# The SwiGLU block of a two-layer hybrid decoder in two phases: gate and up with stationary weight tiles, then down over all of K

## What is computed

```python
h = rms_norm(x, attn_norm_w[l])
proj = h @ w_in[l]
...
x = x + concat([attn, ssm]) @ w_out[l]
h = rms_norm(x, ffn_norm_w[l])
ff = (silu(h @ w_gate[l]) * (h @ w_up[l])) @ w_down[l]
x = x + ff
```

## Time and profile before

| | |
|---|---|
| time, three runs | 2185.56, 2186.34, 2186.9 us |
| median | 2186.34 us |
| span of the profiled execution | 2184.5 us |
| TensorE busy | 2165.0 us (99%), 10150 matmuls |
| VectorE, ScalarE, GpSimd busy | 58%, 46%, 5% |
| DMA read from HBM | 388.43 MB, 179 GB/s over the span |

### The profile page before, as it was taken

One profiled execution on the slowest core, in us unless ns is written; L12 is line 12 of the kernel. 1 busy time (PEld: TensorE's weight loads), 2 busy tenths in 40 slices (PEclk: granted clock), 3 DMA queues, 4 the chain that ended last, 5 costly groups with the idle time before them and its releaser, 6 DMA issues.

```text
span 2184.5 us, 29947 instructions
## 1 busy us (share of the span) xinstructions
PE 2165.0 (99%) x10150; PEld 1794.3 (82%) x10150; DVE 1272.9 (58%) x1542; ACT 1004.1 (46%) x1284; POOL 111.1 (5%) x159
## 2 busy tenths in 40 slices
PE   9999999999999999999999999999999999999998
PEld 7888888888888888888878887888888888888887
DVE  5866765455555555555567666555555555555555
ACT  5555654444444434444355556544444444344442
POOL 2023100000000000000000232000000000000000
PEclk9999999999999999999999999999999999999999
DMA  6554356666656556665545533565665555666654
GB/s 217 174 164 135 116 174 188 192 193 193 190 189 189 189 192 192 192 187 189 174 147 182 159 122 127 182 192 187 191 193 190 191 189 188 191 192 192 187 189 153
DMA packets 202813, 391.55 MB, mean 179 GB/s; under 512 B 12224, under 2 KB 12592, under 8 KB 202736
## 3 DMA queue, kind: packets, MB, share of 16 engines
q1 hardware_dynamic: 201952, 388.67, 55.9%
q0 software_dynamic: 784, 1.90, 0.3%
HBM read 388.43 MB, written 2.10 MB: 179 GB/s over the span
## 4 chain that ended last, share of the span: by engine, by line
PE 97%; ACT 1%; issue 1%; DVE 0%; SPq 0%; POOL 0%; DMA 0%; DVEq 0%; ACTq 0%; POOLq 0%
PE ps L458 91%; PE ps L467 3%; PE ps L557 1%; PE ps L506 0%; PE ps L621 0%; PE ps L620 0%; PE ps L593 0%; PE ps L594 0%; PE ps L619 0%; POOL ys L424 0%; PE ps L565 0%; PE ps L562 0%; PE ps L548 0%; ACT w_hi L770 0%; DMA vrows<-in_k_norm_w_dram 0%
## 5 line engine op out<-in xcount | busy, mean ns | idle before, releaser
L1003 DVE TENSOR_TENSOR w_lo<-raw,w_hi 128x1024 fp32r<-128x1024 f32 x736 | 905.7, 1232 | 739.0 <-ACT w_hi L985 544.4
L985 ACT CAST w_hi<-raw 128x1024 fp32r<-128x1024 f32 x480 | 506.7, 1056 | 739.4 <-PE ps L458 739.4
L458 PE MATMUL ps<-w_hi,h_hi 128*128 128x512 f32 x1984 | 624.0, 396 | 3.6 <-DVE h_lo L1012 3.5
L458 PE MATMUL ps<-w_hi,h_lo 128*128 128x512 f32 x1984 | 613.3, 390 | 0.0
L458 PE MATMUL ps<-w_lo,h_hi 128*128 128x512 f32 x1984 | 612.4, 390 | 0.0
L458 PEld LDWEIGHTS ps<-w_lo,h_hi 128*128 128x128 f32 x1984 | 373.3, 188 | 79.0
L458 PEld LDWEIGHTS ps<-w_hi,h_lo 128*128 128x128 f32 x1984 | 373.3, 188 | 78.8
L458 PEld LDWEIGHTS ps<-w_hi,h_hi 128*128 128x128 f32 x1984 | 366.5, 188 | 75.1 <-DVE w_lo L1003 4.4
L770 ACT CAST w_hi<-raw 128x1024 fp32r<-128x1024 f32 x256 | 269.9, 1055 | 199.9 <-PE ps L458 193.5
L458 PE MATMUL ps<-w_hi,m_hi 128*128 128x512 f32 x960 | 297.2, 391 | 2.6 <-DVE m_lo L1194 2.6
L458 PE MATMUL ps<-w_hi,m_lo 128*128 128x512 f32 x960 | 295.8, 389 | 0.0
(11 more groups left out here) (181 smaller groups left out, 852.5 us busy)
## 6 DMA issues: line engine op xcount, KB each, us to landing
raw<-in_w_gate_dram SPq DMA_DIRECT2D x176, 512.0 KB, 3.5
raw<-in_w_up_dram SPq DMA_DIRECT2D x176, 512.0 KB, 3.5
raw<-in_w_down_dram SPq DMA_DIRECT2D x176, 512.0 KB, 4.3
raw<-in_w_in_dram SPq DMA_DIRECT2D x144, 512.0 KB, 3.4
raw<-in_w_out_dram SPq DMA_DIRECT2D x64, 512.0 KB, 4.2
out_dram<-xr SPq DMA_DIRECT2D x4, 512.0 KB, 2.8
xr<-in_x_dram POOLq DMA_DIRECT2D x3, 512.0 KB, 6.7
xr<-in_x_dram SPq DMA_DIRECT2D x1, 512.0 KB, 4.4
```

The lines of the kernel that those rows point to most:

```text
L458: done = nc.tensor.matmul(ps[:, bank + t, :], lhs[:, rows + k, t * P:(t + 1) * P], w[:, slot, k, :], start=(first and k == 0 and w is w_hi ...
L985: nc.scalar.copy(w_hi[:, s, :, :], raw[:, s, :, :]).then_inc(hi_split, 1)
L1003: v_.tensor_tensor(w_lo[:, slot, :, :], raw[:, slot, :, :], w_hi[:, slot, :, :].bitcast(F32), ALU.subtract).then_inc(lo_split, 1)
```

## The change

- **Gate and up** are formed for all 11 chunks first. The weight tile of 128x128 is stationary and 256 columns of h (all tokens) move: products_turned, 24 matmuls of 256 columns for a pair. The result comes out with inner columns on partitions, so turn_ff and its PSUM use are gone.
- rs now lies along the free axis: two transposes per layer spread it over all partitions (spread_rs), ACT copies it to rsb. DVE multiplies gate by rsb (scale_gate), ACT applies SiLU in place (silu_gate), DVE multiplies up by it (form_ff), ACT copies to f_hi and DVE forms f_lo, each 128x1024. The factor rs of up is applied at the end, when the down sum is added (add_down).
- f_hi and f_lo hold 44 tiles each for all of K. The attention's buffers and m_hi, m_lo lie in the same memory.
- **Down** follows: four output chunks, 22 pairs each, summed over all of K in PSUM, added to x once per output chunk.
- The next layer's transposes of vrows and of x's first three chunks stand between the down pairs, the fourth behind pair 1 of the next layer. SP loads the next layer's parameter rows a chunk before the down phase, and stores each output chunk but the last between the loads of the one after.
- Layers and chunks are written out without hardware loops; thresholds are constants. Each product group alternates between banks 0, 1 and 2, 3 in one count over both layers (bank_of).

```diff
-    P_LOOP = P_FF + 2 * PPG
-    DOWN = DCH * CT // 2
-    PER_FF = 2 * PPG + DOWN
-    P_LAST = P_LOOP + (FCH - 1) * PER_FF
-    PAIRS = P_LAST + DOWN
+    FT = FF // P
+    PER_FF = 2 * PPG
+    P_DOWN = P_FF + FCH * PER_FF
+    DOWN = FT // 2
+    PAIRS = P_DOWN + DCH * DOWN
...
+            def products_turned(slot, pair, rows, bank, first, last):
+                pe.wait_ge(lo_split, pair + (1 + RING))
+                for k in range(2):
+                    for h, w in ((h_hi, w_hi), (h_lo, w_hi), (h_hi, w_lo)):
+                        for m in range(CT):
+                            done = nc.tensor.matmul(ps[:, bank + m // 2, m % 2 * TOK:(m % 2 + 1) * TOK],
+                                                    w[:, slot, k, m * P:(m + 1) * P], h[:, rows + k, :],
...
+                done.then_inc(pair_used, 1)
...
+            def spread_rs(layer):
+                pe.wait_ge(rs_ready, layer * 2 + 2)
+                for t in range(T):
+                    last = nc.tensor.transpose(ps[:, 6, t * P:(t + 1) * P], rs[:, t:t + 1].broadcast_to([P, P]),
+                                               ident[:, :])
+                last.then_inc(rsb_psum, 1)
...
+                for n in range(DCH):
...
                     for q in range(DOWN):
...
+                        if n == 0 and q % 2 == 0:
+                            pe.wait_ge(ff_lo, layer * FCH + (q // 2 + 1))
+                        products(q % RING if n % 2 == 0 else (q + 2) % RING, base + (P_DOWN + n * DOWN + q), 2 * q,
+                                 down_bank(layer, n), f_hi, f_lo, q == 0, q == DOWN - 1)
+                        if layer + 1 < DEPTH and n == 0 and q == 0:
+                            turn_vecs(layer + 1)
+                        if layer + 1 < DEPTH and n and q == 1:
+                            if n == 2:
+                                pe.wait_ge(vec_ready, layer + 2)
+                            turn_x(layer + 1, 0, n - 1)
...
+            def ff_high(layer, c):
+                act.wait_ge(ff_ready, layer * FCH + c + 1)
+                nc.scalar.copy(f_hi[:, CT * c:CT * (c + 1), :],
+                               stage[:, 1].rearrange("p t (a c) -> p (t a) c", a=2)).then_inc(ff_hi, 1)
...
+            def scale_gate(layer, c):
...
+                dve.wait_ge(pair_used, layer * PAIRS + (P_FF + c * PER_FF + PPG + RING))
+                at = gate_bank(layer, c)
+                v_.tensor_tensor(by_tile(stage[:, 0]), by_tile(ps[:, at:at + 2, :]),
+                                 rsb[:, :].unsqueeze(1).broadcast_to([P, CT, TOK]), ALU.mult).then_inc(gate_scaled, 1)
...
+            def form_ff(layer, c):
+
+                dve.wait_ge(pair_used, layer * PAIRS + (P_FF + (c + 1) * PER_FF + RING))
+                dve.wait_ge(gate_silu, layer * FCH + c + 1)
+                at = up_bank(layer, c)
+                v_.tensor_tensor(stage[:, 1], ps[:, at:at + 2, :], stage[:, 0], ALU.mult).then_inc(ff_ready, 1)
```

More of the change, by code:

```diff
@@ L14 @@
+import math
 from contextlib import ExitStack
@@ L255, in load_pair @@
                     .then_inc(raw_landed[slot], 16)
[L257 to L298, removed]
@@ new lines, in _ @@
+            for layer in range(DEPTH):
+                for p in range(PAIRS):
+                    load_pair(p % RING, layer * PAIRS + p, source(layer, p))
+                    if layer == 0 and p == 1:
+                        load_rows(0)
+                    if layer + 1 < DEPTH and p == P_DOWN - PER_FF:
+                        load_rows(layer + 1)
+                    if layer == DEPTH - 1 and p >= P_DOWN + DOWN and (p - P_DOWN) % DOWN == 8:
+                        store((p - P_DOWN) // DOWN - 1)
@@ L351, in _ @@
             pool.memset(numbers[:, 7:8], 0.0).then_inc(const_ready, 1)
-            with pool.Fori(0, DEPTH) as layer:
-                one = bass.ds(layer, 1)
+            for layer in range(DEPTH):
+                one = slice(layer, layer + 1)
                 for dst, src in ((dtb, dt_bias), (alog, a_log), (dskip, d_skip), (sink, sinks)):
@@ L793, in squares @@
                 else:
-                    own.done(layer, ins)
+                    own.done(ins)
             def x_square(layer, i):
@@ L892, in g_hi, with rsb_out @@
                 turned_hi(m_hi, 8 + CT * z, 4, V_SSM + CT * z, gT_psum, layer * 4 + (2 * z + 1), mg_hi)
[L894 to L907 removed]
+            def rsb_out(layer):
+                act.wait_ge(rsb_psum, layer + 1)
+                nc.scalar.copy(rsb[:, :], ps[:, 6, 0:TOK]).then_inc(rsb_ready, 1)
@@ new lines, in _ @@
+            act.wait_ge(vec_psum, 1)
+            own.done(nc.scalar.copy(vecs[:, :], ps[:, 6, 0:VROWS]))
+            nc.scalar.mul(qw[:, :], vecs[:, V_Q:V_Q + 1], HEAD ** -0.5).then_inc(vec_ready, 1)
+            x_hi(0, 0, 0)
+            split(1)
+            x_hi(0, 0, 1)
+            split(2)
+            for layer in range(DEPTH):
+                base = layer * PAIRS
+                for p in range(PAIRS):
+                    if base + p + LEAD < ALL:
+                        split(base + p + LEAD)
+                    if layer == 0 and p in (0, 2):
@@ L990, in _ @@
-                ff_high(layer * 2 * FCH + 2 * FCH - 1)
-                for p in range(P_LAST + LEAD, PAIRS):
-                    split(layer, p)
-            own.check()
+                        x_chunk_squares(layer, 1, (p - 82) // 8)
+                    if P_FF <= p < P_DOWN:
+                        c, q = (p - P_FF) // PER_FF, (p - P_FF) % PER_FF
+                        if c == 0 and q == PPG:
+                            rsb_out(layer)
+                        if q == (PPG + 2 if c == 0 else PPG):
+                            silu_gate(layer, c)
+                        if c and q == 0:
+                            ff_high(layer, c - 1)
@@ new lines, in ff_low @@
+            def ff_low(layer, c):
+                dve.wait_ge(ff_hi, layer * FCH + c + 1)
+                tiles = slice(CT * c, CT * (c + 1))
+                v_.tensor_tensor(f_lo[:, tiles, :], by_tile(stage[:, 1]), f_hi[:, tiles, :].bitcast(F32),
+                                 ALU.subtract).then_inc(ff_lo, 1)
+            split_lo(0)
+            x_lo(0, 0, 0)
+            split_lo(1)
+            x_lo(0, 0, 1)
+            split_lo(2)
+            for layer in range(DEPTH):
+                base = layer * PAIRS
+                for p in range(PAIRS):
```

458 lines of the change are left out of this document (236 added, 222 removed).

## The result

The changed kernel takes **2234.22 us** (median of 4 runs, 2233.18 to 2234.27) against 2186.11 us of the kernel before beside it. The ratio is 1.022, 95% interval 1.0206 to 1.0235: slower by 2.2%, 48 us, where 2158 us was forecast. The profiled execution has a span of 2232.4 us.

A forecast was written before the change was run, and what follows sets the result against it. TensorE, busy 99% of the span, was taken as the bound. 2184.5 - 22.7 - 6.4 + 0.6 + 0.1 = 2156.1 us span; with the runs' median 1.84 us above the span, 2158 us, range 2152 to 2174.

The forecast's parts named there:

- the first term: Gate and up turned: 8448 matmuls of 256 columns cost the same as 4224 of 512, 0 us added.
- turn_ff goes: FFN chunks: eight transposes per chunk leave PE, with the waits at each layer's end, -22.7 us together.
- the boundary: Between the layers: the stall for h_lo and the slow-clock first pair go, transposes stand between down pairs, -6.4 us.
- spread_rs: Two added transposes per layer on PE, with the changes of matmul kind around them, +0.6 us.
- the tail: Last down group: its sum now also multiplies by rs, 747 for 684 ns, twice, +0.1 us.
- the wait at the last chunk: End of each layer's FFN: PE idles 1.28 us for m_lo; with transposes and slow restarts 2.43 us, twice, saved.
- DVE, ACT and the leads: FFN: DVE and ACT stay near half busy, splits run three pairs ahead of PE, so nothing is added.
- The pace of pairs: Gate and up: matmuls 113 to 114 ns apart; prediction wrong if 24 short matmuls take over 2.8 us.
- the short stream can't be fed: Every gate and up chunk: instruction supply can't keep up, 118 ns a matmul, 39 us more, 2197 us; chance 10%.
- pair starts cost: Gate and up: each pair of 24 short matmuls pays 0.03 us at its start, +10.6 us, 2169 us; chance 16%.
- loads bare: Gate and up: each of 4224 added 188 ns weight loads stands on the path, 794 us, 2950 us; chance 1%.
- Exchanges quicken: Attention stages: constant thresholds take away PE's 3.6 us of waits, 2154 us; chance 7%.

The follow-up runs named there:

- experiment 10: Kernel before with each 512-column product made as two of 256 with the same stationary tile: 2294.26 us, ratio 1.0499.
- experiment 4: Changed kernel with f_hi and f_lo moved 96 bytes lower, to a multiple of 128 bytes: 2212.4 us, ratio 1.0124 to the kernel before.
- Experiment 7: Changed kernel with f at a multiple of 128 bytes, but gate and up formed unturned as before: 2175.79 us, ratio 0.9958 to the kernel before.
- experiment 3: Kernel of matmul blocks alone on TensorE, varying address phases and column counts: 128, 320 and 384 columns took 110.8, 146.6 and 174.4 ns.

## Why the prediction was wrong

**The step that failed** is the first term: "So each load lies under the matmul before it, the columns set the pace, and 8448 x 113.35 = 4224 x 226.7: nothing added." Two readings fitted one row. The 512-column pace of 226.7 ns is 213.3 ns of columns at 2.4 GHz and 13.4 ns more; I read these as proportional to the columns because dt_products came out at exactly half. They are a fixed price for each matmul with its load, which four numbers of columns and experiment 10 show. dt_products at 113.3 were in a steady pace that they hold in one kernel and not in another: 118.4 ns in experiment 10, at the same addresses. Gate and up never had it. What chooses that pace stays open. The arithmetic that should have raised doubt stood in the trace: 226.7 less 512 columns leaves 13.4 ns, and a fixed price would have given 120 ns and +56 us. I had bounded this term by +10.6 us beside the forecast and by +39 us in a rival with 10%. The term measured **+56.2 us** for 0.

**A term that was missing.** The diff puts f_hi at 229344 - 2 * FT * TILE, 32 bytes past a multiple of 64 and 96 bytes out of phase with w_hi, and m_hi and m_lo on it. I priced this edit at nothing without naming it. It measured **+22 us** (experiment 4), for w_out as well, which the change does not touch otherwise.

**Point by point.**
- *turn_ff goes, the boundary, spread_rs, the tail: -28.4 us.* Right in sum. With f in phase the changed kernel is 27.8 us above the kernel before, and 56.2 - 28.4 is 27.8; the interval of that comparison is about 4 us to either side, so the exact match is luck. Experiment 7 singles out the boundary and the wait at the last chunk: 9.5 us expected, 8.7 measured (6.3 to 12.2 by the interval). The transposes of turn_ff follow by difference, and no run takes them out alone.
- *DVE, ACT and the leads.* Right: PE waits for no split in the FFN, and DMA releases none of ACT's but the kernel's first.
- *The pace of pairs.* The prediction's own test failed as it said it would: 24 short matmuls take 2.88 us, over the 2.8 named.
- *Rival: the short stream can't be fed (10%).* The side was right, and its price of 118 ns near, but not its mechanism. Matmuls of 128 columns with their loads come every 110.8 ns (experiment 3), so the supply can do at least that. The pace is 120.0 in a block of 96 alone, grows with the columns at 2.4 GHz, and changes to 117.8 with 64 bytes of address.
- *Rival: pair starts cost (16%).* Out as the cause: the blocks alone have no pairs and no waits in them and run at 120.0.
- *Rival: loads bare.* Out: in gate and up PEld is busy 480.00 of 480 us and PE as well, and 120.0 is far from 188 more. The Trainium skill ("TensorE: Matmul & The Clock Gate", Part 3, The mechanism) states that a weight load overlaps running matmuls only when the row groups differ. This trace does not agree: loads of all rows overlap, and what is left on the path is 13.3 ns.
- *Exchanges quicken, at most 3.6 us.* Hardly: PE's waits there are 3.2 us for 3.6. The argument against it, that most end on another engine's work, holds by their number, but 1.9 of the 3.6 us were "issue". The sum of the terms is 1.8 us above the measured span, which is within what the runs of the kernel before differ by.

The mechanism beneath stays open. The pace depends on the phase between the two operands' addresses, 226.7 or 233.3 ns at 512 columns, 120.0, 118.6 or 117.8 at 256. That may point to something that both share, and no run here shows what. The Trainium skill ("TensorE: Matmul & The Clock Gate", Part 2, Step-by-step) says that loading the next tile's weights takes no read bandwidth from the running matmul. No run here measures that bandwidth; that the distance of the two operands' addresses changes the pace by 6.6 ns at 512 columns is not what one would expect from it.

## What to carry to other kernels

Count matmuls and their weight loads as well as columns: in this number format each matmul with its load took about 13 ns beside the columns, so turning a product to save a transpose must not halve the columns per load. Test a pace that is to be multiplied by thousands against two column counts before using it, since one short block may sit in a pace of its own: here the same 32 matmuls ran at 113.3 ns in one kernel and at 118.4 in another. Watch the start addresses of matmul operands, moving and stationary, whenever buffers move: 64 bytes were worth 1% here, in a kernel whose code was the same.

## What the runs showed that was not expected

- In phase (both operands' start addresses the same modulo 256 bytes) a matmul with its own load takes N/2.4 GHz + 13.3 ns: 120.0, 146.6, 174.4 and 226.7 ns for 256, 320, 384 and 512 columns.
- One operand 32 or 64 bytes on: 233.3 ns at 512 columns, worse by 3%, and 117.8 to 118.3 at 256, better by 1 to 2%. 96 bytes out of phase, as f was, took 234.3.
- A stream has more than one steady pace for the same code: one block took 118.3 ns in one kernel and 113.3 in another, and dt_products 113.3 before and 118.4 in experiment 10.
- Stationary columns 16 bytes apart take 232.2 ns at 256 moving columns, about twice the dense ones. 128 moving columns take 110.8 ns (7.09 us for 64 in the set of experiment 3), hardly less than 256. Something other than the columns sets the pace there; that it is the load is likely, and not shown.
